# Expert weights in 64 KB and 32 KB rows instead of 16 KB rows, in a one-core mixture-of-experts layer

## What is computed

```
for e in range(N_EXPERTS):                       # 32 experts
    gu = ht @ w_gate_up[e] + b_gate_up[e]        # 1024 x 2048 weights: 8 MB
    gate, up = gu[:, :D_FF], gu[:, D_FF:]
    gate = jnp.minimum(gate, SWIGLU_LIMIT)
    up = jnp.clip(up, -SWIGLU_LIMIT, SWIGLU_LIMIT)
    act = gate * jax.nn.sigmoid(SWIGLU_ALPHA * gate) * (up + 1.0)
    out = out + combine[:, e:e + 1] * (act @ w_down[e] + b_down[e])   # 1024 x 1024 weights: 4 MB
```

## Time and profile before

| | us |
|---|---|
| median of 3 executions | 1237.35 |
| the profiled execution, its own time | 1237.29 |
| its span in the trace | 1235.4 |
| TensorE (PE) busy | 1160.8 |
| VectorE busy | 420.2 |
| ScalarE busy | 266.9 |
| bytes moved by DMA | 455.25 MB |
| DMA packets | 67292 |

### The profile page before, as it was taken

The page is one execution under the profiler, slowest core; times in us unless marked ns, Lnnn a source line. Parts: engine busy times, 40 slices in busy tenths (PEclk is TensorE's granted clock), DMA queues, the critical chain, the costliest instruction groups (busy, mean ns, idle before and its releaser), DMA issues.

```text
span 1235.4 us, 13704 instructions
## 1 busy us (share of the span) xinstructions
PE 1160.8 (94%) x5828; PEld 599.6 (49%) x5828; DVE 420.2 (34%) x703; ACT 266.9 (22%) x422; POOL 0.2 (0%) x4
## 2 busy tenths in 40 slices
PE   7999999999999999999999889888988898889987
PEld 6899968888533443443343324333433333333332
DVE  6777878756421221222112112111221121111112
ACT  6866546344210000010010001000100010000002
POOL 0000000000000000000000000000000000000000
PEclk9999999999999999999999999999999999999999
DMA  9454425698999999999999999999999999999996
GB/s 322 147 157 151 148 91 171 217 399 340 365 425 428 427 428 428 427 429 425 429 426 429 428 428 428 427 428 428 427 428 425 429 427 429 427 429 427 427 426 263
DMA packets 67292, 455.25 MB, mean 368 GB/s; under 512 B 6970, under 2 KB 23771, under 8 KB 39966
## 3 DMA queue, kind: packets, MB, share of 16 engines
q1 hardware_dynamic: 65654, 454.06, 89.8%
q10 hardware_dynamic: 1576, 0.29, 0.1%
HBM read 453.29 MB, written 1.05 MB: 368 GB/s over the span
## 4 chain that ended last, share of the span: by engine, by line
PE 64%; DMA 32%; DVE 2%; issue 1%; ACT 1%; DVEq 0%; ACTq 0%
DMA ring<-in_w_gate_up 28%; PE bank L1201 18%; PE bank L1219 12%; PE total L902 6%; PE bank L902 5%; PE total L890 4%; PE bank L890 4%; DMA ring<-in_w_down 3%; PE bank L960 2%; PE bank L1187 2%; PE bank L979 1%; PE total L1233 1%; PE total L1201 1%; PE bank L1208 1%; PE total L950 1%
## 5 line engine op out<-in xcount | busy, mean ns | idle before, releaser
L1201 PE MATMUL bank<-ring,hy_area 128*64 128x512 f32 x1984 | 444.6, 595 | 43.2 <-DMA ring<-in_w_gate_up 43.2
L1201 PEld LDWEIGHTS bank<-ring,hy_area 128*64 128x64 f32 x1984 | 136.8, 137 | 331.4 <-issue 244.6
L1219 PE MATMUL bank<-ring,xn_area 128*64 128x512 f32 x992 | 220.1, 595 | 0.3 <-DMA ring<-in_w_down 0.3
L2119 DVE TENSOR_SCALAR qk_area<-bank 128x512 f32<-128x512 f32 x31 | 21.4, 692 | 361.3 <-PE bank L1201 361.3
L1219 PEld LDWEIGHTS bank<-ring,xn_area 128*64 128x64 f32 x992 | 68.4, 137 | 134.6 <-issue 122.8
L1682 ACT ACTIVATE qk_area<-qk_area 128x512 f32<-128x512 f32 x32 | 20.2, 630 | 456.7 <-DVE qk_area L2119 456.7
L2130 DVE SCALAR_TENSOR_TENSOR xn_area_r<-bank,tmp_area,xn_area_r 128x512 fp32r<-128x512 f32 x31 | 23.3, 751 | 200.5 <-ACT xn_area_r L1693 200.5
L1823 DVE TENSOR_TENSOR front_r<-ring,slot_r 128x1024 fp32r<-128x1024 f32 x60 | 73.1, 1222 | 22.2 <-ACT slot_r L1493 22.2
L1493 ACT CAST slot_r<-ring 128x1024 fp32r<-128x1024 f32 x60 | 62.8, 1049 | 43.5 <-PE bank L902 23.2
L1693 ACT ACTIVATE xn_area_r<-bank,tmp_area 128x512 fp32r<-128x512 f32 x31 | 21.3, 687 | 234.9 <-PE bank L1219 221.0
L979 PE MATMUL bank<-tmp_area_r 128*128 128x512 f32 x124 | 38.0, 426 | 12.8 <-issue 8.6
(11 more groups left out here) (397 smaller groups left out, 1253.2 us busy)
## 6 DMA issues: line engine op xcount, KB each, us to landing
ring<-in_w_gate_up SPq DMA_DIRECT2D x116, 2048.0 KB, 37.0
ring<-in_w_down SPq DMA_DIRECT2D x54, 2048.0 KB, 38.9
ring<-in_w_in SPq DMA_DIRECT2D x31, 1024.0 KB, 5.7
ring<-in_w_gate_up SPq DMA_DIRECT2D x22, 1024.0 KB, 9.4
ring<-in_w_down SPq DMA_DIRECT2D x19, 1024.0 KB, 9.9
ring<-in_w_branch_gla SPq DMA_DIRECT2D x4, 1024.0 KB, 5.2
ring<-in_w_branch_hy SPq DMA_DIRECT2D x4, 1024.0 KB, 7.7
ring<-in_w_out SPq DMA_DIRECT2D x4, 1024.0 KB, 6.3
```

What stands on the lines that cost most here:

```text
L1201: last = pe.matmul(to[bk][half * CAP:(half + 1) * CAP, :], xeT[:, j, q, :], where(j, c), start=False, stop=(j == GU_CH - 1), skip_group_ch ...
L1219: last = pe.matmul(banks[to][half * CAP:(half + 1) * CAP, :], half_of(turned, f), where(j, c * D + half * 512), start=(f == 0), stop=(f == ...
L2119: nc.vector.tensor_scalar(gate, made[0][:, :], LIMIT, None, ALU.min).then_inc(gate_ready, 1)
```

## The change

1. **Wider loads.** From expert 8 to expert 28 (`WIDE`), a gate-up matrix is one transfer of eight chunks wherever its eight slots lie side by side in the ring; where they don't, it is one of four chunks and two of two. A down matrix there is one transfer of four chunks. All other loads keep their width.
2. **Features by eights.** So that a row is in one piece in memory, partition p holds features 8p to 8p+7 of gate-up matrices from expert 8 on, and rows 8p to 8p+7 of the down matrices of experts 8 to 28. In the other experts gate-up goes by fours instead of by twos.
3. **What follows from that order.** The gather reads its columns with a stride of 8 elements for experts from 8 on, of 4 for the ones before. `scale_fill` takes another set of columns (`C_N2E`). For experts 8 to 28 `swiglu` writes the activation in another order, and ScalarE copies the turned activation with four copies of 64 partitions (`copy_by_eights`) instead of one of 128.

```diff
+WIDE = (8, E - 3)
+def wide(e):
+    return WIDE[0] <= e < WIDE[1]
+def group_by_eights(g):
+    return QUAD * g >= WIDE[0]
 def expert_loads():
     loads, n = [], 0
     while n < E * CH:
         width = 1 if n < 2 * SLOTS or n >= E * CH - 2 * DN_CH else 2
+        e, j = CHUNK_ORDER[n]
+        if wide(e) and j == 0 and slot_of(n) + GU_CH <= SLOTS:
+            width = GU_CH
+        elif wide(e) and j % 4 == 0 and slot_of(n) + 4 <= SLOTS:
+            width = 4
         loads.append((n, width))
         n += width
...
-        def d_cols(d):
-            return slice(d // 2 * 2 * P + d % 2, (d // 2 + 1) * 2 * P, 2)
+        def d_cols(d, by_eights=False):
+            if by_eights:
+                return slice(d, D, DB)
+            return slice(d // 4 * 4 * P + d % 4, (d // 4 + 1) * 4 * P, 4)
...
-            def rows_of(e, j, width):
-                if j < GU_CH:
-                    r = j // 2 * 2 * P
-                    src = wgu[e, r:r + 2 * P, :].rearrange("(p i) n -> p (i n)", i=2)
+            def rows_of(e, j, width, by_eights=False, down_by_eights=False):
+                if j < GU_CH and by_eights:
+                    at = j
+                    src = wgu[e].rearrange("(p i) n -> p (i n)", i=8)
+                elif j < GU_CH:
+                    r, at = j // 4 * 4 * P, j % 4
+                    src = wgu[e, r:r + 4 * P, :].rearrange("(p i) n -> p (i n)", i=4)
+                elif down_by_eights:
+                    at = j - GU_CH
+                    src = wdn[e].rearrange("(p i) n -> p (i n)", i=8)
                 else:
-                    r = (j - GU_CH) // 2 * 4 * P
+                    r, at = (j - GU_CH) // 2 * 4 * P, j % 2
                     src = wdn[e, r:r + 4 * P, :].rearrange("(p i) n -> p (i n)", i=4)
-                at = j % 2
                 return src[:, at * SLOT:(at + width) * SLOT]
...
+            def copy_by_eights(count):
+                sc.wait_ge(actT_psum, count)
+                src = banks[2][:, :].rearrange("p (c s) -> p c s", c=4)
+                for b in range(2):
+                    for half in range(2):
+                        last = nc.scalar.copy(actT[half * CAP:(half + 1) * CAP, :, b * CAP:(b + 1) * CAP],
+                                              src[b * CAP:(b + 1) * CAP, :, half * CAP:(half + 1) * CAP])
+                last.then_inc(actT_ready, 1)
...
                 if e == E - 1:
                     copy_actT(E, actT_last)
+                elif wide(e):
+                    copy_by_eights(e + 1)
                 else:
                     copy_actT(e + 1, at=2)
...
-                nc.vector.tensor_tensor(act, up, sig, ALU.mult).then_inc(act_ready, 1)
+                if by_eights:
+                    u, g = (m.rearrange("p (m b c) -> p m b c", b=2, c=4) for m in (up, sig))
+                    nc.vector.tensor_tensor(act.rearrange("p (b m c) -> p m b c", b=2, c=4), u, g, ALU.mult).then_inc(act_ready, 1)
+                else:
+                    nc.vector.tensor_tensor(act, up, sig, ALU.mult).then_inc(act_ready, 1)
```

More of the change, by code:

```diff
@@ L88 @@
 C_N2D = C_B2 + 1
-C_ALL = C_N2D + DB
+C_N2E = C_N2D + DB
+C_ALL = C_N2E + DB
 TWO_PI_HI = 6.28125
@@ L768, in moe @@
                 s = slot_of(n)
-                sp.dma_start(ring[:, s * SLOT:(s + width) * SLOT], rows_of(*CHUNK_ORDER[n], width)).then_inc(moe_loaded[s], 16)
+                e, j = CHUNK_ORDER[n]
+                sp.dma_start(ring[:, s * SLOT:(s + width) * SLOT],
+                             rows_of(e, j, width, group_by_eights(e // QUAD), wide(e))).then_inc(moe_loaded[s], 16)
             def moe_aside(k, part):
@@ L959, in gather_fill @@
                             moving = sel4[:, a, :, 0:CAP] if width > CAP else more_sel_r[:, a, 0:CAP]
-                            last = pe.matmul(banks[bank_of][:, i * width:(i + 1) * width], src[:, a, d_cols(d)], moving,
+                            last = pe.matmul(banks[bank_of][:, i * width:(i + 1) * width], src[:, a, d_cols(d, by_eights)], moving,
                                              start=(m == 0 and a == 0), stop=(m == 1 and a == TB - 1))
@@ L1370, in _ @@
                     for k in range(FILLS // 2):
-                        gather_fill(k, 3 - k, QUAD * CAP)
+                        gather_fill(k, 3 - k, QUAD * CAP, group_by_eights(g + 1))
                     pe.wait_ge(xeT_act, 2 * g + 3)
@@ L1666, in _, with scale_fill @@
                             sigmoid_tile(n, a, empty(n))
-            def scale_fill(k, bank_of, width, count, first=False):
+            def scale_fill(k, bank_of, width, count, first=False, c=C_N2D):
                 per = 512 // width
@@ L1674, in scale_fill @@
                     dst = xeT[:, d, :, :].rearrange("p q s -> p (q s)") if width > CAP else xeT[:, d, 0, :]
-                    last = nc.scalar.mul(dst, banks[bank_of][:, i * width:(i + 1) * width], col(C_N2D + d))
+                    last = nc.scalar.mul(dst, banks[bank_of][:, i * width:(i + 1) * width], col(c + d))
                     if first and i == 0:
@@ L2114, in take_weights, with swiglu @@
                 nc.vector.tensor_copy(cslot[:, columns], source).then_inc(cslot_ready, 1)
-            def swiglu(used, count, made=banks[0:2]):
+            def swiglu(used, count, made=banks[0:2], by_eights=False):
                 dve.wait_ge(chunks_used, used)
@@ L2150, in _ @@
                 g, q = e // QUAD, e % QUAD
-                swiglu(PLACE[e, GU_CH - 1] + 1, e + 1, gu_banks(e))
+                swiglu(PLACE[e, GU_CH - 1] + 1, e + 1, gu_banks(e), wide(e))
                 if q == QUAD - 1 and g < GROUPS - 1:
-                    scale_fill(1, FILLS * (g + 1) + 2)
+                    scale_fill(1, FILLS * (g + 1) + 2, C_N2E if group_by_eights(g + 1) else C_N2D)
                 if e < E - 1:
@@ L2212, in vector_columns @@
     parts += [np.concatenate([a[n], a[n]])[None, :] for n in ("hy_freq", "hy_ffn_b1", "hy_ffn_b2")]
-    parts += [a["norm2_w"].reshape(-1, P, 2).transpose(0, 2, 1).reshape(-1, P)]
+    parts += [a["norm2_w"].reshape(-1, P, n).transpose(0, 2, 1).reshape(-1, P) for n in (4, 8)]
     return np.ascontiguousarray(np.concatenate(parts, 0).T)
```

16 lines of the change are left out of this document (8 added, 8 removed).

## The result

| | before | changed |
|---|---|---|
| median, same chip | 1237.26 us (4 runs) | 1255.31 us (4 runs, 1254.36 to 1257.37) |
| ratio | | 1.0145 [1.0133, 1.0157] |
| the profiled execution, and its span | 1237.29 and 1235.4 us | 1255.85 and 1254.0 us |
| TensorE busy | 1160.8 us | 1193.3 us |

The forecast was 1237.1, at most 1242.0. From the page of the changed kernel: packets, the chain's shares, four groups by line (busy, mean ns, idle time before and its cause), two kinds of load (count, KB, us to landing).

A forecast was written before the change was run, and what follows sets the result against it. DMA was taken to bound the experts' part, TensorE the very end. 1237.3 - 5.5 (transfers) + 4.4 (coarse landing) + 0.55 (copies) + 0.2 + 0.1 (strides) = 1237.1 us, no change; 8-in-10 range 1232.5 to 1242.

The forecast's parts named there:

- the strided reads: Gathers' stationary loads at wider strides: 0.2 us more in gate-up 28, 0.1 us ahead of 330 us.
- the queue's running dry: DMA queue at eight-chunk loads: shallow but not empty, 6.3 us in hand, costed at nothing.
- The saving per transfer: Loads up to gate-up 28: 69 fewer transfers at 0.08 us each save 5.5 us (4 to 7).
- The coarse landing and the tail: From gate-up 28's landing TensorE's own work lasts 104.1 us against 99.65 before, giving back 4.4 us.
- my 1121: Forecast start of gate-up 28, in us, in the changed kernel.
- a period of 29.2: Forecast time per expert in us, set by DMA: 29.51 less 0.3.
- The copies: Four copies ahead of downs 8 to 28: 0.55 us each, twenty hidden in waits, expert 28's counted.
- The gathers bind: Rival: gathers at twice their time push group-end experts over the period; 1240.6 us, chance 0.07.
- Cut up: Rival: hardware splits 64 KB rows into 16 KB packets, so nothing is saved; 1242.5 us, chance 0.09.
- read more slowly: Rival: eight-chunk loads read at the slowest row's 420 GB/s, adding 9 us; 1246 us, chance 0.07.
- The saving reaches the end: Rival: 8.3 us saved on transfers, copies and strides wholly hidden; 1233.4 us, chance 0.27.

The follow-up runs named there:

- the loads alone: Kernel before with the changed kernel's wide loads, keeping gathers at stride 2, one copy and the old activation order: 1239.37 us, ratio 1.0015.
- the last kernel with fillers: Kernel of the loads alone plus seven calls of zero-adding matmuls ahead of gate-up 27 only: 1241.36 us, ratio 1.0030.

## Why the prediction was wrong

- **Which steps failed.** Two terms of the sum: the strided reads, put at 0.2 + 0.1 us, and the queue's running dry, put at nothing. Either mistake alone would have cost 2 to 4 us; together they cost 18.
- **The strided reads: wrong, and the start of it all.** I took 10 to 20 ns more per load from L1208, the row at stride 4, as nearest. The same reading at the gather itself takes 327 to 332 ns at a stride of 4 and of 8, and eight matmuls 2.12 us for 1.16. Why L1208's load takes only 208 ns, at what I read as a stride of 4, stays open (it is a transpose of another tile, and no run separates the two); I should have taken the upper bound where one row stood for another operand. In the tail this is 1.9 us where I had 0.2 (my upper bound was 2.3). Ahead of 350 us it is 3.3 where I had 0.1. I never asked what a few us there do in between, where TensorE waits for nothing from 350 to 600 us. The stride of 4 of experts 0 to 7 was the dearer half, and I passed over it in one line.
- I had quoted the Trainium skill, "SBUF — State Buffer", section "Door 1: The DMA port swizzle", with full rate inside lines of 16 bytes and float32 strided for free up to 4. The runs agree with the lines: with two elements in each (stride 2) a gather's matmuls follow each other every 0.12 us, with one in each (strides 4 and 8) every 0.24. They don't agree with a free stride of 4, and the measurement decides.
- **The queue: nearly right in its size, wrong in its use.** Of the 6.3 us in hand 5.3 were there. I checked that TensorE's pace per expert is under DMA's in the steady state, and not whether TensorE is in time at the first wide expert: it came 10.2 us late. The sum had "cost at nothing, cover 6.3 us" and needed the cover's own state. With pairs the strides cost 3 to 4 us, with loads of four chunks the time is 2 us above the kernel before, with eights 18.
- **The saving per transfer: right for the four-chunk loads** (0.07 to 0.08 us). With eights, the loads alone had gained some 4.2 us by 1150 where I had 5.5: 1.2 in bytes moved, 2.2 that the additional holes took, and 0.8 by which DMA was late at 350 us already. By the landing of gate-up 29's last pair, 2.4 us earlier than before, it is 4.6.
- **The coarse landing and the tail: right.** After gate-up 28 starts, TensorE does not wait for weights, and the stretch takes 103.6 us with the loads alone (104.1 in the sum). What sets gate-up 28's start was wrong: I had its landing, and in the changed kernel it is TensorE's own work from gate-up 27 on.
- **The sum once more, to gate-up 28's start** (17.6 us late against my 1121). Gate-up 27 starts as its load lands, at 1106.58, where 1121 less a period of 29.2 gives 1091.8: 14.8 us. Of these some 4.2 are the start's lateness, as DMA shows it at 540 us, and 9.5 the additional idle time; some 1.1 remain that the counts don't settle. The other 2.8 us are TensorE's expert 27, 32.0 us instead of 29.2: the slowed clock costs it 1.75, the strided gathers 2.0 and the copies 0.55, less the 1.5 by which an expert that is last of its group was under the period. I had no term for the clock.
- **The copies: right** (0.53 us each), hidden, as the run of them alone shows.
- **The rivals.** *The gathers bind* named the mechanism and priced it at 3.5 us, because it counted only the last group. *Cut up* is refuted by the packets, which are whole rows, and *read more slowly* by their times: one of 64 KB takes 2420 ns, two of 32 KB 2426. *The saving reaches the end* needed a queue that is never idle.

## What to carry to other kernels

Widening transfers in a ring is paid in depth of queue: before costing that at nothing, follow the consumer's lateness from the first wide load, not only its pace in the steady state, and compare it with the microseconds in hand. A side effect of a new layout (here the stride of a gather) must be costed at every place where it runs, the early ones first, and two costs that are each small with the old code may multiply. If a change has several grains, try the part that has no side effect first.

## What the runs showed of the hardware

- Reading float32 operands at wide strides is slow on three engines. On TensorE, against a stride of 2, a stationary load goes from 196 to 327 ns at a stride of 4 and 332 at 8. At a stride of 8 ScalarE's pass over 1024 elements goes from 1150 to 2188 ns, and VectorE's from 1275 to 2219 ns.
- After a wait of some us TensorE's granted clock is at half for a stretch (0.50 at 750 to 755 us, that is 1.2 GHz), and a gate-up of 13.9 us takes 15.4 to 16.9. It followed waits of 0.9 to 8.0 us, though not each: behind one of 3.48 us (ahead of a gate-up at 595.37, in the last kernel with fillers) the next took 13.95. Where matmuls filled the wait ahead of gate-up 27 the clock stayed at 2.4 GHz (1.00 at 1098 to 1104 us in the last kernel with fillers).
- A packet may be a whole row of 64 KB: 1792 packets of the changed kernel are, 128 for each of its 14 eight-chunk loads, and the median one takes 2420 ns.
